# Every second copy of transposed probabilities moves from ScalarE to VectorE in a sparse-attention loop

## What is computed

```python
scs = einsum("bghqd,bgqkd->bghqk", qc, kg) * scale      # selected branch; the windowed one has this form too
p = masked_softmax(scs, mask)
o_sel = einsum("bghqk,bgqkd->bghqd", p, vg)
o = gates[..., 0:1] * o_cmp + gates[..., 1:2] * o_sel + gates[..., 2:3] * o_win
return o.reshape(b, s, NSA_Q_DIM) @ w_out
```

## Time and profile before

| | |
|---|---|
| median of 3 runs | 2327.48 us (2324.46 to 2328.87) |
| the profiled execution's own time | 2324.71 us |
| its span, first to last instruction | 2323.0 us |
| mean granted TensorE clock | 0.957 of full speed |
| busy share over the span | PE 94%, weight loads 76%, DVE 56%, ACT 35%, POOL 13% |
| attention loop | from about 122 us to 360 us of the span |

### The profile page before, as it was taken

One profiled execution on the slowest core, in us unless ns is written; L12 is line 12 of the kernel. 1 busy time (PEld: TensorE's weight loads), 2 busy tenths in 40 slices (PEclk: granted clock), 3 DMA queues, 4 the chain that ended last, 5 costly groups with the idle time before them and its releaser, 6 DMA issues.

```text
span 2323.0 us, 27345 instructions
## 1 busy us (share of the span) xinstructions
PE 2185.6 (94%) x10704; PEld 1761.7 (76%) x10704; DVE 1309.9 (56%) x2222; ACT 818.9 (35%) x1324; POOL 292.7 (13%) x201
## 2 busy tenths in 40 slices
PE   8999988999999899997789899999989999999997
PEld 6866666788888678876678688888778877888885
DVE  4277654767754577638884487764445545333333
ACT  4156653544332253423242353442122223222221
POOL 0000001000049500002310200009800000000000
PEclk9999989999999899998799899999979998999998
DMA  8110002232346223320003133226503322323331
GB/s 259 58 46 20 19 10 64 88 94 91 98 154 201 91 91 98 93 91 10 1 1 106 49 109 100 91 86 213 181 28 109 92 81 64 91 92 99 86 98 52
DMA packets 59791, 203.58 MB, mean 88 GB/s; under 512 B 6800, under 2 KB 7312, under 8 KB 59408
## 3 DMA queue, kind: packets, MB, share of 16 engines
q1 hardware_dynamic: 55920, 191.36, 26.6%
q10 hardware_dynamic: 3744, 10.49, 1.4%
HBM read 197.63 MB, written 2.10 MB: 86 GB/s over the span
## 4 chain that ended last, share of the span: by engine, by line
PE 75%; POOL 10%; DVE 6%; ACT 4%; issue 3%; DMA 1%; POOLq 0%; SPq 0%; DVEq 0%; ACTq 0%
PE bank L645 21%; PE bank L646 21%; PE bank L647 21%; POOL ada_acc L553 5%; POOL ada_w L550 3%; PE bank L600 2%; POOL h L535 2%; ACT pbuf L1216 1%; PE bank L746 1%; DVE pbuf L1646 1%; PE bank L841 1%; PE bank L795 1%; PE bank L818 1%; ACT whi L1076 1%; PE bank L627 1%
## 5 line engine op out<-in xcount | busy, mean ns | idle before, releaser
L645 PE MATMUL bank<-xhi,whi 128*128 128x512 f32 x1712 | 688.8, 402 | 28.6 <-DVE xlo L1425 22.7
L646 PE MATMUL bank<-xlo,whi 128*128 128x512 f32 x1712 | 683.6, 399 | 0.0
L647 PE MATMUL bank<-xhi,wlo 128*128 128x512 f32 x1712 | 683.0, 399 | 0.0
L1413 DVE TENSOR_TENSOR wlo<-raw,whi 128x1024 fp32r<-128x1024 f32 (+1 forms) x322 | 414.1, 1286 | 391.9 <-ACT whi L1076 391.9
L1076 ACT ACTIVATE whi<-raw 128x1024 fp32r<-128x1024 f32 (+1 forms) x322 | 334.6, 1041 | 814.7 <-PE bank L647 758.4
L645 PEld LDWEIGHTS bank<-xhi,whi 128*128 128x128 f32 x1712 | 325.8, 190 | 110.2 <-DVE xlo L1425 12.9
L647 PEld LDWEIGHTS bank<-xhi,wlo 128*128 128x128 f32 x1712 | 325.4, 190 | 80.2
L646 PEld LDWEIGHTS bank<-xlo,whi 128*128 128x128 f32 x1712 | 326.0, 190 | 77.6
L645 PE MATMUL bank<-hid_hi,whi 128*128 128x512 f32 x528 | 211.6, 401 | 0.0
L646 PE MATMUL bank<-hid_lo,whi 128*128 128x512 f32 x528 | 210.4, 398 | 0.0
L647 PE MATMUL bank<-hid_hi,wlo 128*128 128x512 f32 x528 | 210.2, 398 | 0.0
(11 more groups left out here) (269 smaller groups left out, 2571.1 us busy)
## 6 DMA issues: line engine op xcount, KB each, us to landing
raw<-w SPq DMA_DIRECT2D x298, 512.0 KB, 3.6
ada_w<-w_ada SPq DMA_DIRECT2D x64, 384.0 KB, 3.2
raw<-w SPq DMA_DIRECT2D x24, 384.0 KB, 3.3
h<-xT ACTq DMA_DIRECT2D x8, 256.0 KB, 9.3
w_k<-w_cmp ACTq DMA_DIRECT2D x1, 2048.0 KB, 10.6
w_v<-w_cmp ACTq DMA_DIRECT2D x1, 2048.0 KB, 8.7
out_t<-h ACTq DMA_DIRECT2D x8, 256.0 KB, 2.0
dk<-stg ACTq DMA_DIRECT2D x2, 256.0 KB, 7.2
```

Of the source, the lines that this page charges most:

```text
L645: pe.matmul(bk, whi[w][:, cols], hi[:, k, :], start=k == 0, stop=False)
L646: pe.matmul(bk, whi[w][:, cols], lo[:, k, :], start=False, stop=False)
L647: return pe.matmul(bk, wlo[w][:, cols], hi[:, k, :], start=False, stop=last)
L1413: dve.tensor_tensor(wlo[g % SLOTS][:, 0:n], raw[g % RAWS][:, 0:n], whi[g % SLOTS][:, 0:n].bitcast(F32), ALU.subtract).then_inc(s_lo, 1)
```

## The change

The copies of units 1 and 3 of a step leave ScalarE. VectorE makes them with `tensor_copy`: unit 1 between `out_low(i-2)` and `masked(i+2)`, unit 3 after `masked(i+2)`. These are 40 of 88 copies: two of 512 columns in step 0, two of 384 in step 1, one of 512 in step 3. `turn_bank_free` and `pv` wait for one semaphore of each engine.

```diff
-        USERS += ["turn"] * len(turned_units(_i))
+        USERS += [("turn", "turn_v")[_u % 2] for _u in range(len(turned_units(_i)))]
...
             if n >= 2 and USERS[n - 2] == "turn":
-                eng.wait_ge(s_tk, turns_to(n - 1))
+                eng.wait_ge(s_tk, USERS[:n - 1].count("turn"))
+            elif n >= 2 and USERS[n - 2] == "turn_v":
+                eng.wait_ge(s_tv, USERS[:n - 1].count("turn_v"))
...
             def pv(s):
-                pe.wait_ge(s_tk, turns_through(s))
+                n = TURN_AT[s] + len(turned_units(s)) + (s % 4 == 0)
+                pe.wait_ge(s_tk, USERS[:n].count("turn"))
+                pe.wait_ge(s_tv, USERS[:n].count("turn_v"))
...
                 for u, gs in enumerate(turned_units(s)):      # ScalarE
                     at_ = TURN_AT[s] + u
+                    if u % 2:
+                        continue
...
+            def keep_turned(s, u):                            # VectorE
+                n, units, at_ = (step_of(s)[1] + 1) * P, turned_units(s), TURN_AT[s] + u
+                if u >= len(units):
+                    return
+                gs = units[u]
+                dve.wait_ge(s_T, turns_to(at_ + 1))
+                if s >= 2:
+                    dve.wait_ge(s_pv, s - 1)
+                dve.tensor_copy(pt[:, s % 2, gs[0]:gs[-1] + 1, 0:n],
+                                turn_bank(at_)[:, 0:len(gs) * n].rearrange("p (g n) -> p g n", n=n)).then_inc(s_tv, 1)
...
                 if i >= 2:
                     out_low(i - 2)
+                if 0 <= i < STEPS:
+                    keep_turned(i, 1)
                 if i + 2 < STEPS:
                     masked(i + 2)
+                if 0 <= i < STEPS:
+                    keep_turned(i, 3)
```

More of the change, by code:

```diff
@@ L168, in turns_to @@
 def turns_to(n):
-    return USERS[:n].count("turn")
+    return USERS[:n].count("turn") + USERS[:n].count("turn_v")
 def turns_through(s):
@@ L378, in build @@
         s_T = sem("probs_turned")
-        s_tk = sem("turned_kept")
+        s_tk = sem("turned_kept_act")
+        s_tv = sem("turned_kept_dve")
         s_cs = sem("compressed_scores_made")
```

## The result

| | before | after |
|---|---|---|
| median | 2325.97 us (4 runs, 2323.67 to 2328.87) | 2348.78 us (4 runs, 2347.56 to 2349.58) |
| ratio | | 1.0097, 95% interval 1.0079 to 1.0114 |
| span of the profiled execution | 2323.0 us | 2347.8 us |
| mean granted TensorE clock | 0.957 | 0.950 |

The changed kernel is 22.8 us slower. The forecast was 2341.5 us with a range of 2332 to 2351, so the sign and the range hold, and the likeliest time was 7 us too low. New lines push the numbers up a little: the masking is now L1653 and L1656, the first instruction of `scaled` L1663, `out_low` L1727, the transposes L821, the compressed scores L809, `pv` L846 and L851, ScalarE's copy L1240, its exponentials L1221, the new copy on VectorE L1718.

A forecast was written before the change was run, and what follows sets the result against it. A chain round PE, VectorE and ScalarE, none full, sets the period. Step 3's 6.2, step 1's 4.4 and the tail's 1.7 make 12.3; with 1.65 for the clock 2338.7, plus 2.8 to the median: 2341.5 us, range 2332 to 2351.

The forecast's parts named there:

- The load reading: Reading set against the forecast's: VectorE is the busier helper, so a copy costs 0.61 or 0.47 us wherever it stands.
- Price of a copy: On VectorE: 0.693 us for 512 columns, 0.55 for 384; 0.61 and 0.47 us to the next instruction.
- the low bound of 8 us: Sum if VectorE's copies were as short as its scaling inside SBUF, about 0.4 us apart: 8 us.
- Step 3: Unit 1's copy ahead of `masked` delays it 0.94 us a period: 0.33 waiting for transposes, 0.61 copying.
- step 0: Unit 3's transposes wait for unit 1's bank, +0.23 us; unit 3's copy is covered by VectorE's idle time.
- step 1: Compressed scores wait for VectorE's copy of unit 3: +0.54 us a period, including 0.23 carried from step 0.
- The first period's 1.34: Step 1 in the first period, where VectorE is later against ScalarE: the new copy ends 1.34 us later.
- Tail: Loop's end without filler: +0.61 us in iteration 27, then +1.7 us in all through iterations 28 and 29.
- The clock: One more period with PE partly at half clock, +1.65 us; none and five such stretches were the bounds.
- Rival A: Slower by much, 2350 us: five more half-clock stretches of 1.65 us each, slow stretches becoming frequent; chance 0.2.
- B: Faster, about 2322 us: two engines empty the turn banks at once in steps 0 and 1, saving 5.6 us; chance 0.05.
- C: No difference, 2327 us: VectorE's delays are absorbed because it idles 7.5 us in a period; chance 0.08.

The follow-up runs named there:

- the faster version: Kernel before, with only step 0's units 0 and 1 copied by VectorE, ahead of `scaled`: 2317.49 us, ratio 0.9962.
- moving the panel alone: Kernel before, all copies on ScalarE, weight panel's high half made behind step 0's copies from the second period on: 2321.06 us, ratio 0.9967.
- PE kept busy: Changed kernel plus unused matmuls ahead of step 1's compressed scores, six in the first period, three in each of the next five: 2343.73 us, ratio 1.0063.

## Why the forecast was right in direction and too low in size

- **What bounds the loop.** Right. The chain goes round all three engines, and none of them is full. The load reading is refuted by moving a single copy with VectorE's load unchanged (26.98 against 27.92), and once more by the version that is faster with a busier VectorE.
- **Price of a copy.** Right: 693 and 548 ns, and 0.61 us in the queue, measured alone at 27.06 - 26.45. So the low bound of 8 us for the sum falls, and so does the high one: the second wait ahead of `pv` shows no cost, since periods come to 27.91 to 27.93.
- **Step 3, step 0, step 1.** Forecast 0.94, 0.23 and 0.31 (0.54 less the carried 0.23); measured 0.94, 0.23 and 0.31, each with the others left out. The first period's 1.34 is confirmed where it ran at full clock (28.35).
- **Tail.** Forecast 0.61 + 1.7 = 2.3, measured 4.2. A `pv` at half clock (2.83 against 1.53 us) explains 1.3 of the difference; the rest was not taken apart.
- **The clock: this is the term that failed.** The forecast had one more stretch at 1.65 us. Against full-clock lengths, in the first six periods it was 3.3 us in the first, 1.3 in the second, 1.4 in the fourth, less the 1.65 that before lost in one of its own: 4.3 us net. With last period and tail the loop is 7.0 us above the 12.3 of work and waits, where 1.65 stood. The error of reasoning was to price a stretch by the one that before shows, and to count on full clock because five of six periods had it. The forecast itself had the compressed scores of the first period come 1.34 us later (PE's idle time ahead of them grew from 0.73 to 1.58 us), and did not ask what that does to the clock. What the clock does with such a gap isn't settled by the runs either: half clock followed it in three executions and not in a fourth, of another kernel.
- **Rival A** (2350 us, chance 0.2) was partly right: about 20 to 27 us more at half clock than before, and a median nearer to its time than to the likeliest one's. But not every such stretch costs time. The sixth period ran at a granted 0.94 in 27.90 us, no longer than its neighbour at 1.00, with PE busy for 25.97 us in place of 24.55: PE was slower where it would have waited.
- **Rivals B and C.** Refuted where the change puts the copies. B's mechanism, two engines emptying the banks, is not what helps even in the faster version: there VectorE makes both copies of the pair, and moving the panel alone gains as much.
- **The rest of the 24.8 us.** 1.1 ahead of the loop and 4.5 behind it. Over the twelve profiles the stage behind the loop lay between 1981.3 and 1989.7 us, with the unchanged kernel at both ends but for 0.3 us; I hold this for chance. The start of the loop lay between 120.8 and 123.5 us. It was 122.4 in both executions of before, and 123.5 and 123.3 in those of after, with no moved copy ahead of it; that difference is not explained.

**Open.** Which idle times cause the other stretches at half clock in the loop (174, 232, 283, 314, 338 and 358 us) wasn't tried one by one, and why half clock follows a gap of 1.58 us in one kernel and not in another isn't known. With PE kept busy the first stretch in the loop begins at 254 us. What sets the clock behind the loop wasn't tried either.

## What to carry to other kernels

An engine with idle time is not free to take work: what an added instruction costs is set by what stands behind it in that engine's order, and by whether its input is there when its turn comes. Look for the place, not for the less busy engine: the same copy cost 0.94 us a period ahead of the masking and nothing behind it, and a pair of them gained 1.1 us where VectorE was idle and ScalarE came late. Where the chain has a gap on PE, ask for the clock before adding to it, and before moving work off ScalarE, see whether ScalarE only does it in the wrong order.

## What the runs showed of the hardware

- With additional matmuls in a gap of PE of 1.58 us, whose result nobody reads, a loop took 234.5 us in place of 238.6. In the kernel without them half clock followed the gap for about 6.8 us and cost 3.3 us. In another kernel full clock followed a gap of 1.57 us.
- The stretches at half clock can repeat: in two executions of the changed kernel they began at the same seven times, to some 0.2 us, and the loops agree to 0.01 us. In two of the kernel before only the stretch that begins near 298 us was common, and the loops differ by 2.6 us.
- Half clock does not always cost: a period with a granted 0.94 was as long as one with 1.00 (27.90 and 27.91 us).
